# One core, Trainium2: the modulation of the first later block by row products on VectorE beside the hyena branch, and an attention loop that turns its probabilities one step later

## The reference, cut to what matters

```python
# second layer of the first block: attention and hyena from the same input
p_lat = u_lat @ w_in
q_l = axial_rope(split_q(p_lat[..., :C_QK], g_q[i]), ang_row, ang_col)
...
s = jnp.einsum('bqhjd,bkhjd->bhjqk', q, k) * (C_HEAD_DIM ** -0.5)
p = jax.nn.softmax(s, axis=-1)
a = p[:, :, 0] - lam * p[:, :, 1]
return jnp.einsum('bhqk,bkhe->bqhe', a, v)
...
y_hy_lat = hyena_mixer(p_lat[..., hy_cols], conv_d[i], filt_lat, hf_bias[i])
y_lat = jnp.concatenate([diff_head_out(o_lat, ...), y_hy_lat], axis=-1) @ w_out_cd[i]
# each later layer i
cond = jax.nn.silu(c)
mod = cond @ ada_w[i] + ada_b[i]          # 1024 -> 6144
```

## Time and profile before

| | |
|---|---|
| median of 3 runs | 2946.55 us (2942.25 to 2948.18) |
| the profiled execution | 2940.45 us, span 2938.0 us |
| TensorE busy | 2645.0 us of the span |
| VectorE busy | 1268.8 us |
| ScalarE busy | 956.3 us |
| granted TensorE clock, mean | 0.97 |
| moved by DMA | 796.14 MB |

### The profile page before, as it was taken

One profiled execution on the slowest core, in us unless ns is written; L12 is line 12 of the kernel. 1 busy time (PEld: TensorE's weight loads), 2 busy tenths in 40 slices (PEclk: granted clock), 3 DMA queues, 4 the chain that ended last, 5 costly groups with the idle time before them and its releaser, 6 DMA issues.

```text
span 2938.0 us, 34279 instructions
## 1 busy us (share of the span) xinstructions
PE 2645.0 (90%) x13172; PEld 1705.1 (58%) x13172; DVE 1268.8 (43%) x2206; ACT 956.3 (33%) x1778; POOL 39.3 (1%) x51
## 2 busy tenths in 40 slices
PE   8999887877889889878788899999999999999999
PEld 3444432222465363222225699887898988985787
DVE  1752300001232430000014688657877457764676
ACT  3112310101122330000003555546555445544443
POOL 0010000000000000000000000000000000000000
PEclk9999999999999999999999999989999999999999
DMA  8674499999931749999992478614867517852152
GB/s 364 279 308 171 171 427 429 429 429 429 428 114 63 291 196 393 428 429 429 428 428 111 164 295 325 242 58 162 337 245 278 192 72 301 317 234 86 69 189 100
DMA packets 59492, 796.14 MB, mean 271 GB/s; under 512 B 8636, under 2 KB 9916, under 8 KB 10748
## 3 DMA queue, kind: packets, MB, share of 16 engines
q1 hardware_dynamic: 55664, 790.13, 66.0%
q10 hardware_dynamic: 3724, 4.59, 0.5%
HBM read 793.64 MB, written 1.05 MB: 270 GB/s over the span
## 4 chain that ended last, share of the span: by engine, by line
PE 73%; DMA 18%; DVE 4%; ACT 3%; issue 2%; SPq 0%; ACTq 0%; DVEq 0%; POOL 0%; POOLq 0%
PE banks L1977 12%; PE banks L2001 9%; DMA ring<-in_t_gate 9%; PE banks L1492 8%; DMA ring<-in_t_up 6%; PE banks L915 6%; PE banks L800 5%; PE banks L930 5%; PE banks L1508 3%; PE banks L767 3%; DMA ring<-in_t_down 2%; PE banks L1994 2%; PE banks L1367 2%; PE banks L787 2%; PE banks L1620 1%
## 5 line engine op out<-in xcount | busy, mean ns | idle before, releaser
L1492 PE MATMUL banks<-ring,arena 128*64 128x512 f32 x1920 | 476.3, 621 | 103.3 <-DMA ring<-in_t_up 56.4
L1492 PEld LDWEIGHTS banks<-ring,arena 128*64 128x64 f32 x1920 | 161.0, 143 | 396.3 <-issue 351.7
L2387 ACT CAST w_hi<-ring 128x1024 fp32r<-128x1024 f32 x256 | 268.4, 1055 | 315.1 <-PE banks L1977 166.4
L3021 DVE TENSOR_TENSOR ring_lo<-ring,w_hi 128x1024 fp32r<-128x1024 f32 x256 | 313.1, 1224 | 133.9 <-ACT w_hi L2387 131.6
L2593 DVE TENSOR_TENSOR arena<-arena,banks 128x512 f32<-128x512 f32 x32 | 22.0, 688 | 795.2 <-PE banks L1492 795.2
L2001 PE MATMUL banks<-u_pair,w_hi 128*128 128x256 f32 x1536 | 278.9, 284 | 3.7 <-DVE ring_lo L3021 3.1
L2109 ACT COPY arena<-banks 32x512 f32 x96 | 55.3, 576 | 606.5 <-PE banks L1508 605.8
L2001 PEld LDWEIGHTS banks<-u_pair,w_hi 128*128 128x128 f32 x1536 | 240.2, 192 | 6.6 <-DVE ring_lo L3021 3.7
L1508 PE MATMUL banks<-ring,arena 128*64 128x512 f32 x896 | 205.2, 612 | 28.3 <-DMA ring<-in_t_down 16.0
L2001 PE MATMUL banks<-u_pair,ring_lo 128*128 128x256 f32 x768 | 217.5, 283 | 0.0
L1977 PE MATMUL banks<-w_hi,ffn_h_hi 128*128 128x512 f32 x512 | 201.1, 393 | 0.0
(11 more groups left out here) (370 smaller groups left out, 4021.1 us busy)
## 6 DMA issues: line engine op xcount, KB each, us to landing
ring<-in_t_ffn SPq DMA_DIRECT2D x64, 2048.0 KB, 8.4
ring<-in_t_gate SPq DMA_DIRECT2D x60, 2048.0 KB, 22.0
ring<-in_t_up SPq DMA_DIRECT2D x60, 2048.0 KB, 22.1
ring<-in_t_down SPq DMA_DIRECT2D x56, 2048.0 KB, 21.3
ring<-in_t_ada SPq DMA_DIRECT2D x36, 2048.0 KB, 13.8
ring<-in_t_ada_dots SPq DMA_DIRECT2D x36, 2048.0 KB, 9.1
ring<-in_t_ret_in SPq DMA_DIRECT2D x12, 2048.0 KB, 7.9
arena<-in_t_down SPq DMA_DIRECT2D x8, 2048.0 KB, 32.0
```

What stands on the lines that cost most here:

```text
L1492: mm = nc.tensor.matmul(PS[64 * h:64 * h + 64, f.bank, :], x_cur[:, b, k, :], wview(un[h0 + h], KC)[:, k, :], start=(k == 0), stop=(k == K ...
L2387: nc.scalar.copy(w_hi[:, n % 4], w).then_inc(S("ffn_w_hi"), 1)
L3021: TT(w_lo, w, w_hi[:, n % 4].bitcast(F32), ALU.subtract).then_inc(S("ffn_w_lo"), 1)
```

## The change

The modulation matrix of the first later layer moves from the tiles laid out by rows (`t_ada`) to the tiles laid out by outputs (`t_ada_dots`). Its 12 tiles are loaded among those of `cd_norm`'s successors, and VectorE takes its 48 row products in six places of the hyena part. The condition is laid out as a row first: eight transposes by TensorE into banks 0 and 1, and two copies by VectorE. The attention loop loses the modulation and turns the probabilities of step i in step i + 1, the head's output another step later.

```diff
+            fills("cd_cb", [0, 1])
...
+            hy_units, dot_units = load(turn(3), units_of(a["t_in_cd"], 4, 5, 3)), []
+
+            def load_dots(lo, hi):
+                dot_units.extend(load(turn(hi - lo), units_of(a["t_ada_dots"][0], *range(lo, hi))))
+                for t in range(lo, hi):
+                    dot_units[t].used = Mark(S("cd_dot"), 4 * (t + 1))
+
+            load_dots(0, 5)
+            qk_units = load(turn(1), units_of(a["t_in_cd"], 0))
+            load_dots(5, 8)
+            qk_units = qk_units + load(turn(1), units_of(a["t_in_cd"], 1))
+            v_units = load(turn(1), units_of(a["t_in_cd"], 2))
+            load_dots(8, 12)
+            use_dense("hy_in", hy_units, 4, [0, 1, 2, 3] * 3)
...
-            shared = fills("da_shared", [6] * 16)
...
-            fills("b0_rows", [7] * 12)
-            plan["b0_tiles"] = load(turn(12), units_of(a["t_ada"][2], *range(12)))
...
+            fills("da_out", [6] * 4)
@@ TensorE
                 norm_pe(pe, c, "cd_norm", 2, wait=False)
+                cond_row_pe(pe, "cd_cb")
...
-                for i in range(8):
+                for i in range(10):
                     if i < 7:
                         scores(i + 1)
-                    tiles = DA_TILES[i]
-                    ada_rows_pe(plan["b0_tiles"][tiles[0]], plan["b0_rows"][tiles[0]])
-                    turn_probs(i)
-                    b0_cols(tiles[0])
-                    for t in tiles[1:]:
-                        ada_rows_pe(plan["b0_tiles"][t], plan["b0_rows"][t])
-                    if i % 2:
-                        out_head(i // 2)
-                    for t in tiles[1:]:
-                        b0_cols(t)
+                    if i >= 3 and i % 2:
+                        out_head((i - 3) // 2)
+                    if 1 <= i <= 8:
+                        turn_probs(i - 1)
@@ ScalarE
                     if i < 7:
                         exps(i + 1)
...
-                    turn_act(i)
...
+                    if 1 <= i <= 8:
+                        turn_act(i - 1)
+                    if i >= 3 and i % 2:
+                        f = plan["da_out"][(i - 3) // 2]
+                        copy_act(act, f, da_o[:, (i - 3) // 2, :], PS[:, f.bank, 0:N])
@@ VectorE
                 norm_dve(dve, c, "cd_norm", 1, 0, 2, x_first=True)
+                for half, f in enumerate(plan["cd_cb"]):
+                    f.full.wait(dve)
+                    V_.tensor_copy(cd_cond[:, half * 512:half * 512 + 512], PS[:, f.bank, :]).then_inc(f.free.sem, 1)
...
+                def cd_dots(lo, hi):
+
+                    for n in range(lo, hi):
+                        u = dot_units[n // 4]
+                        if n % 4 == 0:
+                            u.landed.wait(dve)
+                        w = ring[:, u.slot, (n % 4) * D:(n % 4 + 1) * D]
+                        STT(w, w, 1.0, cd_cond, ALU.mult, ALU.mult, accum_out=MOD[:, 192 + n:193 + n])\
+                            .then_inc(S("cd_dot"), 1)
...
                     if g < 2:
                         hyena_arg(g)
+                    cd_dots((0, 6, 12)[g], (6, 12, 16)[g])
...
+                cd_dots(16, 20)
...
+                cd_dots(20, 24)
                 for m, f in enumerate(plan["hy_out"]):
...
+                cd_dots(24, 48)
                 qk_norm(0, 4)
...
-                b0_dve(DA_TILES[i][0])
...
-                plan["b0_cols"][-1].free.wait(dve)
+                dve.wait_ge(S("cd_dot"), 48)
```

More of the change, by code:

```diff
@@ L149, in weight_tiles @@
     return {
-        "t_ada": stack([by_rows(m) for m in (*np.asarray(w["w_ada"]), np.asarray(w["ada_w_2"])[0])]),
-        "t_ada_dots": stack([by_outputs(m) for m in np.asarray(w["ada_w_2"])[1:]]),
+        "t_ada": stack([by_rows(m) for m in np.asarray(w["w_ada"])]),
+        "t_ada_dots": stack([by_outputs(m) for m in np.asarray(w["ada_w_2"])]),
         "t_gate": experts(w["w_gate"], columns),
@@ L512, in block_program @@
             plan_norm("cd_norm")
+            fills("cd_cb", [0, 1])
             fills("hf_mlp", [4, 5])
             fills("hf_tok", [6, 7])
-            use_dense("hy_in", load(turn(3), units_of(a["t_in_cd"], 4, 5, 3)), 4, [0, 1, 2, 3] * 3)
+            hy_units, dot_units = load(turn(3), units_of(a["t_in_cd"], 4, 5, 3)), []
[10 more added lines that the diff above has]
+            use_dense("hy_in", hy_units, 4, [0, 1, 2, 3] * 3)
             fills("hf_freq", [4, 5, 6, 7])
@@ L519, in block_program @@
             fills("hy_out", [4, 5] * 2)
-            use_dense("qk_in", load(turn(2), units_of(a["t_in_cd"], 0, 1)), 4, [6, 7, 0, 1, 2, 3, 6, 7])
-            use_dense("v_in", load(turn(1), units_of(a["t_in_cd"], 2)), 4, [4, 5, 4, 5])
+            use_dense("qk_in", qk_units, 4, [6, 7, 0, 1, 2, 3, 6, 7])
+            use_dense("v_in", v_units, 4, [4, 5, 4, 5])
             fills("qk_ms", [0, 1, 2, 3] * 2)
@@ L525, in block_program @@
             fills("da_turn", [4, 5] * 4)
-            shared = fills("da_shared", [6] * 16)
-            plan["da_out"] = [shared[4 * h + 3] for h in range(4)]
-            plan["b0_cols"] = [f for n, f in enumerate(shared) if n % 4 != 3]
-            fills("b0_rows", [7] * 12)
-            plan["b0_tiles"] = load(turn(12), units_of(a["t_ada"][2], *range(12)))
-            for u, f in zip(plan["b0_tiles"], plan["b0_rows"]):
-                u.used = f.full
+            fills("da_out", [6] * 4)
             fills("da_sub", [4, 5])
@@ L596, in block_program @@
             if more:
-                fa = lambda q: (SLOT, lambda it, v=a["t_ada_dots"][i], q=q: v[it * 3 + q])
+                fa = lambda q: (SLOT, lambda it, v=a["t_ada_dots"][i + 1], q=q: v[it * 3 + q])
                 items = [f1(0), fa(0), f1(1), fa(1), f2(0), fa(2), f2(1)]
@@ L1086, in turn_pe, with cond_row_pe @@
                         mm.then_inc(f.full.sem, 1)
-        def cond_row_pe(pe, i):
-            for half, f in enumerate(plan[f"b{i}_cb"]):
+        def cond_row_pe(pe, name):
+            for half, f in enumerate(plan[name]):
                 f.open(pe)
@@ L1247, in block_program @@
         hy_t = region(W + 9856, [2, 512])
-        hy_y = region(W + 15200, [4, N])
-        b0_store = region(W + 14080, [2, 512])
-        DA_TILES = [list(range(3 * (i // 2) + 2 * (i % 2), 3 * (i // 2) + 2 * (i % 2) + 2 - i % 2)) for i in range(8)]
+        hy_y = region(W + 14080, [4, N])
+        cd_cond = region(W + 15872, [D])
         da_const = region(W, [768])
@@ L1257, in block_program @@
         da_sq = region(W + 6912, [8, 512])
-        da_rs = region(W + 11008, [8, 512])
+        da_rs = [region(W + 11008 + N * i, [N]) for i in range(4)] + [region(W + 12032 + 512 * i, [512]) for i in range(4)]
         da_p = region(W + 6912, [2, 2, 512])
@@ L2037, in _ @@
                 if i in DOTS:
-                    cond_row_pe(pe, i)
+                    cond_row_pe(pe, f"b{i}_cb")
                 turn_pe(pe, c, f"b{i}_fnorm")
@@ L2176, in _ @@
                         for i in range(4 * t, 4 * t + 4):
-                            rsqrt_act(act, c, plan["qk_ms"][i], N if i < 4 else 2 * N, 64, dst=da_rs[:, i, :])
+                            rsqrt_act(act, c, plan["qk_ms"][i], N if i < 4 else 2 * N, 64, dst=da_rs[i])
                 def exps(i):
@@ L2697, in _ @@
                 norm_dve(dve, c, "cd_norm", 1, 0, 2, x_first=True)
+                for half, f in enumerate(plan["cd_cb"]):
+                    f.full.wait(dve)
+                    V_.tensor_copy(cd_cond[:, half * 512:half * 512 + 512], PS[:, f.bank, :]).then_inc(f.free.sem, 1)
+                plan["cd_cb"][0].free.wait(dve)
+                plan["cd_cb"][1].free.wait(dve)
+                def cd_dots(lo, hi):
[6 more added lines that the diff above has]
+                            .then_inc(S("cd_dot"), 1)
                 def hyena_arg(r):
@@ L2761, in qk_norm @@
                         STT(da_qk[:, i, 0:width], da_qk[:, i, 0:width], col("g_q" if i < 4 else "g_k"),
-                            da_rs[:, i, 0:width], ALU.mult, ALU.mult).then_inc(S("qk_n"), 1)
+                            da_rs[i], ALU.mult, ALU.mult).then_inc(S("qk_n"), 1)
                 def qk_rope(lo, hi):
@@ L2786, in da_max @@
                         TS(stat8[:, 16 + k:17 + k], stat8[:, k:k + 1], -0.125, None, ALU.mult).then_inc(S("da_nb"), 1)
-                def b0_dve(t):
-                    cols_dve(plan["b0_cols"][t], 192 + 4 * t, 0, 2, 1)
                 dve.wait_ge(S("qk_rope"), 8)
@@ L2795, in _ @@
                         da_max(i + 1)
-                    if i >= 1:
-                        for t in DA_TILES[i - 1][1:]:
-                            b0_dve(t)
                     f0, f1 = plan["da_scores"][2 * i:2 * i + 2]
```

2 lines of the change are left out of this document (removed).

## The result

| | before | after |
|---|---|---|
| median | 2945.43 us (2942.25 to 2948.18, 4 runs) | 2925.65 us (2924.51 to 2927.5, 4 runs) |
| ratio | | 0.9935, 95% interval 0.9922 to 0.9947 |
| profiled execution, span | 2938.0 us | 2923.8 us |
| granted clock, mean | 0.97 | 0.965 |

The change is faster by 19.8 us on the medians, where 19.5 were forecast. Between the two profiled executions the difference is only 14.6 us (2940.45 and 2925.82).

The account below looks back on a forecast made before the run. TensorE's path was taken to bound the kernel up to the DMA-bound expert stage. Terms -33.7 + 7.3 + 5.3 + 1.6 = -19.5 us, from 2946.55 to 2927.0 us; range 2916 to 2938.

Parts of the forecast that it names:

- What bounds: TensorE's path up to the experts, then DMA; whatever moves the first expert product (1098.87) moves the end by as much.
- A: Condition's row in the hyena part: `hy_in` waits for banks 0 and 1, then starts at low clock: +7.3 us.
- B: Row products ahead of the filter's decay on VectorE, 1.15 us each, make the filter transforms wait: +5.3 us.
- The first rival: Row products at half rate, 2.3 us each, in VectorE's hyena queue: slower by 13 us, 2960 us; chance 0.03.
- C: The other 32 row products: four make `hy_out` wait, the last 24 are hidden before the query norms: +1.6 us.
- Late tiles: Last three modulation tiles land as late as 25 us, query norms slip some 10 us: -9.5, 2937 us; chance 0.06.
- The loop: Attention loop without modulation, VectorE setting a step of 3.15 us: 34.7 us instead of 68.4, gain 33.7 us.
- The second rival: Clock stays low in the sparse attention loop: loop 46.7 us, total -7.5, 2939 us; chance 0.08.

Follow-up runs that it names:

- all three mended: Changed kernel with condition's row in banks 4 and 5, row products 12 to 15 behind the filter's decay, 20 to 23 behind `hy_out`: 2911.49 us.

## Why the prediction was right

The forecast of 2927.0 lies 1.4 us from the measured 2925.65, and the gain of 19.5 against 19.8. By its steps:

- **What bounds.** The expert stage begins 17.5 us earlier and ends 17.9 earlier. That the shift of its start passes whole into a DMA-bound stage held. DMA is idle ahead of it in the changed kernel too (share 0.00 from 1072 to 1075), as it must be if all slots are full, and with all three mended the stage again begins and ends earlier by one amount, 15.6 us against the changed kernel.
- **A.** 7.3 forecast, 7.6 measured: 6.7 of waiting and 0.9 of low clock in the first tile, where 6.6 and 0.7 were forecast. Moving the banks took the wait away. The 0.9 depends on which tile before it is compared with: behind the same wait of 2.69 us it took 15.74 us in the profile before and 14.05 in that of the later turn alone.
- **B.** 5.3 forecast (the two terms written down, 4.6 and 0.6, give 5.2), 5.5 measured: 4.6 of waiting and 0.95 of slower products. The row product's price, 1.15 from the nearest row, was 1.146 with 0, 4 and 8 in front. The first rival is refuted by it and by the timeline: no product took 2 us. The rule of the Trainium skill that stood behind it ("Vector Engine (DVE) Microarchitecture Reference", section 7) does not hold for this form here: the products follow one another every 1.15 us, and the trace decides.
- **C.** 1.6 forecast, 1.5 measured. The 24 last products ended at 944, within the 941 to 949 forecast, and the query norms came at 957 (954 forecast, plus the shift of 2.6 ahead of the stage). Late tiles played no part: the largest gap in the 24 is 0.02 us.
- **The loop.** 34.7 us forecast, 32.2 measured, near the bound of 31.7 at full clock. VectorE's step without a wait was 3.04 and not 3.15, and the last difference ended 26.8 us behind the first scores (27.2 forecast). The clock was 0.89 on average, about what was assumed; but I had charged it in proportion. It was low at the start and in the tail (0.72 from 990 to 996, 0.83 from 1008 on), and full between, so it cost 1 us of the tail and little else, where 3.0 were charged. Two steps of that working were loose. The time of 27.2 us for the last difference holds the eighth difference, 1.5 us, which its terms don't name. And the head of 3.42 us was only in part at the low clock: a head takes 3.75 us where the clock stays low.
- **The second rival**, a loop at the low clock, did not come true here, but in the old order it did: 63.5 us.
- **What cancels.** The total is closer than its terms: the loop was 2.2 us better, and the pieces outside the stage's terms, low clock for the most part, took 7 us in the profiled pair, whose gain is 14.6 us and not 19.5. The measured terms add up to 21.3 us, so on the medians only 1.5 us would be left for those pieces; no profile shows it. The agreement within 0.3 us is luck; that of A, B and C, each within 0.3 us, was worked out term by term and is not.
- **What the argument did not see.** The prediction priced the removed work and the later turn only together, and doesn't say what either is worth alone; what was expected of the later turn alone, a loop of 56 to 61 us, was too much. Alone they bring 4.7 and 4.4 us in the loop; together they bring 35.9. The loop's number was close because the loop that is left was timed anew, engine by engine, and not by subtracting what was taken out. Had the change been only the first half, the same arithmetic would have said 49 to 52 us at full clock, as it did for that experiment, and the loop took 63.5.

The best version that came out is the one with all three mended: 2911.49 us, 1.2% under the kernel before. It needs one other pair of banks and two row-product calls in other places.

## What to carry to other kernels

When work is taken out of a loop that waits, time the loop that is left from its longest engine: work that lay in a wait gives little back (4.7 us here), and a reordering that removes the wait gives little while other waits take its place (4.4 us). Filler work that is moved into an in-order queue belongs behind the instruction that another engine waits for; each piece ahead of it costs its whole duration once the idle time there is used up. And a helper that borrows a PSUM bank should borrow one whose next user is late.

## What the runs showed of the hardware that was not expected

Taking work off TensorE slowed the rest of it. In the attention loop in its old order, without the modulation, with waits of 3.2 us a step, the mean granted clock was 0.68 where it had been 0.95, heads took 3.75 us in place of 1.96, and 16 useless products made the loop 11 us shorter. Outside such loops the same instructions behind the same wait run at either clock in profiles of kernels that are alike up to there: 7.67 to 10.48 us for eight sums of squares behind 3.1 us, 14.05 or 15.74 for the first tile behind 2.69. Behind the longer waits all profiles agree: 16.6 to 16.9 us for the tile behind 8.47. Together such pieces made 7 us of difference between the profiles before and after, more than the 1.5 us of one of the terms of the sum.
